# Two chained transformer blocks on one core: shift and scale slots by pairs, later first-stage products as rounded pairs

## Chip, core and metric

The kernel runs on one NeuronCore of a Trainium2 chip. The metric is the device time of one execution in microseconds (us). What the text calls engines: TensorE (PE; its weight loads are PEld), VectorE (DVE), ScalarE (ACT), GpSimd (POOL, nearly unused), and SyncE (SP), which here only issues DMA transfers of weights. The core has one PSUM, used as four units of two banks, and one SBUF.

## What is computed

Two blocks for 256 tokens of width 1024, in float32. The part that the change touches is the head of the first block: the modulation vectors, the first norm, and the product with `w_in`.

```python
cs = silu(c)
mod = cs @ mod_w + mod_b                       # six vectors of 1024
sh1, sc1, g1, sh2, sc2, g2 = split(mod, 6)
h = rms_norm(x, norm1_g) * (1 + sc1) + sh1
z = h @ w_in + b_in                            # queries, keys, values, gates, merge gates
...                                            # three attention branches from z
x = x + g1 * (merged @ w_out)
h = rms_norm(x, norm2_g) * (1 + sc2) + sh2
x = x + g2 * moe_ffn(h)                        # 32 experts, 4 per token
x = rms_norm(x, final_g)
...                                            # second block: adaln with 9 vectors for each of 2 layers,
                                               # ffn, neighbourhood attention, ffn, ffn, short convolution, ffn
```

## The kernel before

All activations of a stage lie transposed, 8 chunks of 128 features by 256 tokens (`xT`, `hT`). Weights stream through a ring of slots of 128 x 2048 float32 (1 MB each); `PLAN` writes down the order of the slots, which place of the ring each takes, and what releases that place. SP walks this list in order, and a slot whose place is not released holds up all behind it. In the first stage the ring has 9 places (`RING1`), then 7.

**Modulation slots.** 96 slots hold `mod_w`. Each carries two of the eight 128-row chunks of one vector. `mod_slot(i)` on VectorE multiplies the slot with the condition row (L1860, two instructions with an accumulated sum for one condition, four for two conditions), and after the fourth slot of a vector `modulation(n)` adds the bias, and for a scale the one and the norm's gain (L1879, L1881). The first eight slots are the shift and the scale of the first norm. The next twelve are put one behind each slot of the first stage, 8 in attention, 4 in the branch stage, the others in the feed-forwards of the second block.

**First stage.** `norm(0)`: ScalarE squares `xT` (L758), TensorE sums with a matrix of ones (L1306), ScalarE takes the root (L761). VectorE does eight modulation slots, the reciprocal (L1896), divides four chunks at once (L1936), and scales and shifts each (L1943). Then TensorE runs three passes z0, z1, z2 of 8, 8 and 5 output chunks (`Z_PASSES`) with plain float32 matmuls (`gemm`, L1180), each over 8 input chunks, 168 matmuls in all. VectorE brings each pass out of PSUM with the bias (L1966). Then come transposes of the value chunks ("vnat", L1334), four pieces of 2 output chunks each (`piece`, "zpiece0" to "zpiece3", L1345, 16 matmuls each), and between them the compression network (L1358 to L1407).

**Rounded products.** Later stages split a float32 operand into a rounded part (fp32r, "high", a ScalarE copy) and the rest ("low", a VectorE subtraction) and add three products: high x high, high x low, low x high. In attention the merge pieces do this (`split_piece`, L1468 to L1471; copies L850 and L2047), with `h1_high` (L798) and `h_low`, which lies on top of `hT` (L2052). The experts do it with L898 and L2276, and the second block with `split_gemm` (L1226, copies L1041 and L2412).

**After attention.** The branch stage multiplies each branch by `w_branch` (L1180), VectorE merges it (L2146 to L2151), then `w_out`, which VectorE adds to `xT` (L2167). After the experts, norm2 sums two products (L1306, L1308) with `gains2`, a 128 x 1024 table; VectorE needs its result at L2424.

Of the kernel before, what the change touches and what calls it, by code (L numbers as in the profile page):

```python
# [72 lines left out]
FIRST_VECS = VEC_AT["b_in"][0]  # L73
# [5 lines left out]
for _name, _width in CONSTS:  # L79
# [10 lines left out]
MODS = [(1, 0, g, 1) for g in range(6)] + \  # L90
       [(2, layer, g, 2 if (layer, g) < (0, 5) else 1)
        for layer in range(2) for g in ((0, 1, 2, 5, 6, 3, 7, 4, 8) if layer == 0 else range(N_MOD))]
# [34 lines left out]
class Plan:  # L127
# [3 lines left out]
    def __init__(self):  # L131
# [8 lines left out]
        self.split_at, self.split_no = [], {}  # L140

# [19 lines left out]

    def gemm(self, name, tensor, index, k_chunks, col0, cols, n_units, mods_every=0, mods_end=0, split=False,
             first=0):


# [3 lines left out]
        for k in range(0, k_chunks, 2):  # L169
            self.slots[name].append(len(self.stream))  # L170
# [5 lines left out]
            if split:  # L176
                self.split_no[len(self.stream)] = len(self.split_at)
                self.split_at.append(len(self.stream))
            self.stream.append((tensor, index, (k + first) % k_chunks, 2, col0, cols))
# [5 lines left out]
    def piece(self, name, z):  # L185

        self.unit(name)
        self.slots[name] = len(self.stream)
# [3 lines left out]
    def mod_slots(self, n):  # L192

        for _ in range(n):
            block_, layer, g, _ = MODS[self.n_mod_slots // 4]
            pair = self.n_mod_slots % 4
# [6 lines left out]
def make_plan():  # L203
    p = Plan()
    p.mod_slots(8)
    p.unit("norm0")
    for n, (c0, nc_) in enumerate(Z_PASSES):
        p.gemm(f"z{n}", "w_in", 0, DC, c0 * P, nc_ * P, 2, mods_every=1, mods_end=5)
    p.unit("vnat", 2)
    p.load("cmp_w1", [("cmp_w1", kv, 8 * half, 8, 0, 256) for kv in range(2) for half in range(2)])  # L210
    p.piece("zpiece0", 8)
# [3 lines left out]
    p.piece("zpiece1", 10)  # L215
    p.unit("cmp_hturn")
    p.piece("zpiece2", 12)
# [3 lines left out]
    p.piece("zpiece3", 14)  # L221
# [50 lines left out]
    p.unit("norm2")  # L272
    for e, (f, _) in enumerate(FFNS):
# [57 lines left out]
def square_parts(n):  # L331
# [3 lines left out]
    if n == 2:  # L335
        return PAIRS_OF
# [33 lines left out]
def build(nc, ins, out):  # L370
    with ExitStack() as ctx:
# [92 lines left out]
        gateT, b2_rows, gains2 = area(ARENA - T, T), cond_rows[:, 0, :], area(moe["h_nat_low"][0], D)  # L464
# [30 lines left out]
        w_low = sb_at("w_low", [P, RING2, SLOT], F32R, ring_at)  # L495
        w_high = sb_at("w_high", [P, HIGHS, SLOT], F32R, ring_at + 4 * RING2 * SLOT)
# [51 lines left out]
        def low_ap(s, cols):  # L548
            return w_low[:, PLAN.place[s], 0:2 * cols].rearrange("p (k n) -> p k n", k=2)

# [133 lines left out]
        def _(sp):  # L684
# [7 lines left out]
            stream(0, 3)  # L692
            sp.dma_start(xT[:, :, :], ins["xT"].rearrange("(k p) t -> p k t", p=P)).then_inc(sem("x_landed"), 16)
            stream(3, 10)
            sp.dma_start(vecs[:, FIRST_VECS:], ins["vecs"][:, FIRST_VECS:]).then_inc(sem("rest_landed"), 16)
            sp.dma_start(consts[:, P:], ins["consts"][:, P:]).then_inc(sem("rest_landed"), 16)
            stream(10, PLAN.moe_slot)
# [1980 lines left out]
```

## Time and profile before

| | us |
|---|---|
| median of 3 runs | 2763.68 (2761.77 to 2766.82) |
| the profiled execution, its own time | 2760.82 |
| span from first to last instruction | 2759.0 |
| PE busy | 2640.4 (96%) |
| DVE busy | 2096.0 (76%) |
| ACT busy | 1579.1 (57%) |
| mean granted TensorE clock | 0.98 |

The page cuts the span into 40 equal slices of 69 us. A digit is the busy share in tenths: PE shows 5 in the first slice and 9 in almost all that follow, with 8 in a few. A timeline row gives the start, the busy time of a run of instructions, engine, line and operation, and in square brackets how long the engine had been idle before it and what released it. A window row gives, for a stretch of time, the busy time of each engine, the granted clock (1.00 is 2.4 GHz, 0.50 is 1.2 GHz), the DMA share and GB/s. TensorE's float32 matmuls leave two records each.

### The profile page before, as it was taken

What the parts mean: (1) busy time and instruction counts of PE and PEld (TensorE: products, weight loads), DVE (VectorE), ACT (ScalarE), POOL (GpSimd) and SP (SyncE); (2) the same over time, 40 slices, a digit from 0 to 9 for tenths busy, and PEclk for the clock granted to TensorE, in tenths of its full rate; (3) what the DMA queues carried; (4) which work ended last, traced back from release to release, by engine and by line L of the source; (5) the groups of instructions that cost most, each with busy time, mean ns of one, the idle gap of its engine ahead of it and who ended that gap; (6) DMA issues with size and microseconds to landing.
All of it is one profiled execution on the core that took longest, in us unless ns stands there. A gap on an engine that the chain in (4) does not pass through costs nothing.

```text
span 2759.0 us, 43009 instructions
## 1 busy us (share of the span) xinstructions
PE 2640.4 (96%) x17218; PEld 2403.7 (87%) x17218; DVE 2096.0 (76%) x1998; ACT 1579.1 (57%) x1411; POOL 0.4 (0%) x6
## 2 busy tenths in 40 slices
PE   5999989999999999999998999999989999999998
PEld 4788878888888888888886999999879999999998
DVE  6357749999999999999997888785546866754553
ACT  1145328888888888888884443453434444442442
POOL 0000000000000000000000000000000000000000
PEclk9999999999999999999998999999999999999999
DMA  9844448999999999999995877777417867754551
GB/s 398 292 159 135 177 164 354 378 389 384 394 391 388 393 388 393 391 389 392 387 382 231 279 277 268 287 265 251 144 62 260 289 227 278 287 171 153 175 192 62
DMA packets 160816, 777.62 MB, mean 282 GB/s; under 512 B 12304, under 2 KB 38032, under 8 KB 97456
## 3 DMA queue, kind: packets, MB, share of 16 engines
q1 hardware_dynamic: 156352, 768.71, 73.0%
q10 hardware_dynamic: 4336, 7.05, 0.9%
q8 instruction: 99, 1.62, 0.2%
q14 instruction: 29, 0.24, 0.0%
HBM read 774.66 MB, written 1.05 MB: 281 GB/s over the span
## 4 chain that ended last, share of the span: by engine, by line
PE 79%; DVE 12%; issue 4%; ACT 3%; DMA 2%; SPq 0%; DVEq 0%; ACTq 0%
PE psum L1226 38%; PE psum L1578 18%; PE psum L1180 7%; DVE w_low L2276 6%; PE psum L1618 4%; PE psum L1555 2%; PE psum L1596 2%; ACT w_high L898 1%; PE psum L1306 1%; PE psum L1345 1%; DVE arena L2303 1%; PE psum L1393 1%; PE psum L1440 1%; DVE ring L1860 1%; PE psum L1468 1%
## 5 line engine op out<-in xcount | busy, mean ns | idle before, releaser
L2276 DVE TENSOR_TENSOR w_low<-ring,w_high 128x2048 fp32r<-128x2048 f32 x396 | 884.8, 2286 | 30.1 <-ACT w_high L898 17.7
L898 ACT ACTIVATE w_high<-ring 128x2048 fp32r<-128x2048 f32 x396 | 736.0, 1905 | 43.0 <-PE psum L1578 42.8
L1041 ACT ACTIVATE w_high<-ring 128x2048 fp32r<-128x2048 f32 (+1 forms) x199 | 362.4, 1829 | 527.8 <-PE psum L1226 409.6
L2412 DVE TENSOR_TENSOR w_low<-ring,w_high 128x2048 fp32r<-128x2048 f32 (+1 forms) x199 | 432.6, 2184 | 293.5 <-ACT w_high L1041 292.4
L1226 PE MATMUL psum<-h_high,w_high 128*128 128x256 f32 x2080 | 585.5, 282 | 20.9 <-ACT h_high L1054 20.8
L1226 PE MATMUL psum<-h_high,w_low 128*128 128x256 f32 x2080 | 592.4, 285 | 0.0
L1226 PE MATMUL psum<-h_low,w_high 128*128 128x256 f32 x2080 | 586.7, 284 | 0.0
L1226 PEld LDWEIGHTS psum<-h_high,w_high 128*128 128x128 f32 x2080 | 398.6, 192 | 23.2 <-issue 22.6
L1226 PEld LDWEIGHTS psum<-h_high,w_low 128*128 128x128 f32 x2080 | 394.8, 190 | 0.0
L1226 PEld LDWEIGHTS psum<-h_low,w_high 128*128 128x128 f32 x2080 | 394.1, 190 | 0.0
L1578 PE MATMUL psum<-w_high,xg 128*128 128x512 f32 x1056 | 295.8, 402 | 0.6 <-ACT xg L926 0.6
L1578 PE MATMUL psum<-w_low,xg 128*128 128x512 f32 x1056 | 291.4, 397 | 1.1
L1226 PE MATMUL psum<-m_high,w_high 128*128 128x256 f32 x880 | 245.9, 279 | 1.8 <-DVE arena L2447 1.8
L1860 DVE SCALAR_TENSOR_TENSOR ring<-ring,cond_rows 128x1024 f32<-128x1024 f32 x192 | 228.1, 1221 | 24.9 <-DMA ring<-in_mod_w 14.1
L1226 PE MATMUL psum<-m_high,w_low 128*128 128x256 f32 x880 | 246.2, 280 | 0.0
L1226 PE MATMUL psum<-m_low,w_high 128*128 128x256 f32 x880 | 246.1, 280 | 0.0
L1578 PEld LDWEIGHTS psum<-w_low,xg 128*128 128x128 f32 x1056 | 196.9, 188 | 55.5 <-DVE w_low L2276 8.2
L1578 PEld LDWEIGHTS psum<-w_high,xg 128*128 128x128 f32 x1056 | 196.5, 189 | 45.0 <-issue 0.8
L1578 PE MATMUL psum<-w_high,hid 128*128 128x512 f32 x528 | 152.2, 410 | 23.2 <-DVE hid L2319 23.2
L1226 PEld LDWEIGHTS psum<-m_high,w_high 128*128 128x128 f32 x880 | 165.4, 188 | 2.3 <-DVE arena L2447 2.3
L1226 PEld LDWEIGHTS psum<-m_high,w_low 128*128 128x128 f32 x880 | 165.4, 188 | 0.0
L1226 PEld LDWEIGHTS psum<-m_low,w_high 128*128 128x128 f32 x880 | 165.3, 188 | 0.1
(289 smaller groups left out, 3357.8 us busy)
## 6 DMA issues: line engine op xcount, KB each, us to landing
ring<-in_exp_w SPq DMA_DIRECT2D x396, 1024.0 KB, 8.6
ring<-in_ffn_w SPq DMA_DIRECT2D x135, 1024.0 KB, 5.6
ring<-in_mod_w SPq DMA_DIRECT2D x96, 1024.0 KB, 6.2
ring<-in_ffn_w SPq DMA_DIRECT2D x40, 768.0 KB, 4.9
ring<-in_w_in SPq DMA_DIRECT2D x24, 1024.0 KB, 9.6
ring<-in_even_w_in SPq DMA_DIRECT2D x12, 1024.0 KB, 7.3
ring<-in_conv_w_in SPq DMA_DIRECT2D x12, 1024.0 KB, 5.1
ring<-in_w_branch SPq DMA_DIRECT2D x6, 1024.0 KB, 5.0
```

The costliest lines, as they stand in the source:

```text
L898: act.activation(high_ap(j, D), slot_ap(PLAN.moe_slot + j), ACT.Copy).then_inc(sem("expert_high_ready" + c.x), 1)
L1041: act.activation(high_ap(m, cols), slot_ap(s, 2, cols), ACT.Copy).then_inc(sem("w_high_ready"), 1)
L1180: mm = pe.matmul(unit(u0 + j // 4)[:, (j % 4) * T:(j % 4 + 1) * T], w[:, k % 2, (c0 + j) * P:(c0 + j + 1) * P], rhs(k), start=(k == 0 and ...
L1226: return pe.matmul(unit(u0 + j // 4)[:, (j % 4) * T:(j % 4 + 1) * T], w[:, k % 2, j * P:(j + 1) * P], h[:, k, :], start=first, stop=stop, ...
L1306: mm = pe.matmul(unit(u)[:, 0:T], ones, squares[:, k, :], start=(k == 0), stop=(k == DC - 1))
L1555: mm = pe.matmul(cols[:, n, :, part * CAP:(part + 1) * CAP], h_nat[:, b, k * P:(k + 1) * P], sel[:, b, :, :], start=(b == 0), stop=(b == T ...
L1578: mm = pe.matmul(u[:, cols], x_parts(k), w[:, k % 2, cols], start=(k == 0 and w is wh), stop=(k == DC - 1 and w is wl), skip_group_check=True)
L1596: mm = pe.matmul(u[:, k * CAP:(k + 1) * CAP], moe_buf(rows)[:, k * P:(k + 1) * P], const("fold"), start=True, stop=True)
L1618: mm = pe.matmul(c.unit(name)[:, (k % 4) * T:(k % 4 + 1) * T], moe_buf(f"y_rows{e}")[:, k * P:(k + 1) * P], moe_buf(f"selT{e}"), start=(e ...
L1860: last = dve.scalar_tensor_tensor(to, w[:, j, :], 1.0, cond_rows[:, row, :], ALU.mult, ALU.mult, accum_out=sums)
L2276: dve.tensor_tensor(low_ap(PLAN.moe_slot + j, D), slot_ap(PLAN.moe_slot + j), high_ap(j, D).bitcast(F32), ALU.subtract).then_inc(sem("expe ...
L2412: dve.tensor_tensor(low_ap(s, cols), slot_ap(s, 2, cols), high_ap(m, cols).bitcast(F32), ALU.subtract).then_inc(sem("w_split"), 1)
```

## The change

Four edits, and their consequences for the ring and the order.

**Head.** The shift and scale slots are no longer vector by vector but pair by pair: slot 2p is the shift and slot 2p+1 the scale of input chunks 2p and 2p+1. Each slot is finished by its own small `modulation`, and chunk pair p of `hT` is divided, scaled and shifted right after it and signalled (`h0_parts`). A slot of z0 is streamed behind each two modulation slots. `xT` is now the first transfer on SP. On ScalarE the transfer of the condition comes third and not first; the squares come in four parts before the Silu, and a root of a constant is put ahead of the real one.

**z1, z2 and the four pieces** are three rounded products. Highs of weights are ScalarE copies into the places 9, 10 and 11 of the ring; lows are VectorE subtractions in the slot's own place (`early_lows`). `h1_high` is made in four parts behind `h0_parts`; `h_low` overwrites `hT`, so VectorE waits for the end of z0. Each low is written out at a fixed place of VectorE's order. zpiece0 moves ahead of the vnat transposes.

**Four modulation slots fewer** lie ahead of attention (16 and not 20). Attention keeps its 8, and the branch stage and `w_out` have 8 and not 4. The order of vectors is changed: the gate of the expert block now comes last of these and the second block's first two before it.

**gains2** moves to two other buffers in two halves; one of them is where slots with two conditions leave their products, and the first modulation slot of the second block comes three weight slots later (`since_mods = -2`).

```diff
-MODS = [(1, 0, g, 1) for g in range(6)] + \
+MODS = [(1, 0, g, 1) for g in range(5)] + [(2, 0, 0, 2), (2, 0, 1, 2), (1, 0, 5, 1)] + \
...
+MOD_SLOTS = [(i % 2, i // 2) if i < 8 else divmod(i, 4) for i in range(4 * len(MODS))]
...
 def make_plan():
     p = Plan()
-    p.mod_slots(8)
     p.unit("norm0")
     for n, (c0, nc_) in enumerate(Z_PASSES):
-        p.gemm(f"z{n}", "w_in", 0, DC, c0 * P, nc_ * P, 2, mods_every=1, mods_end=5)
+        p.gemm(f"z{n}", "w_in", 0, DC, c0 * P, nc_ * P, 2, mods_every=2, mods_end=4 if n else 0,
+               highs=((), (9, 10, 11, 9), (10, 11, 9, 10))[n], mods_before=0 if n else 2)
+    p.piece("zpiece0", 8, (9,))
...
+    p.since_mods = -2
...
-            act.dma_start(cond_rows[:, 0, :], ins["cond_rows"][0]).then_inc(sem("cond_landed"), 16)
             act.dma_start(vecs[:, 0:FIRST_VECS], ins["vecs"][:, 0:FIRST_VECS]).then_inc(sem("vecs_landed"), 16)
             act.dma_start(ones, ins["consts"][:, 0:P]).then_inc(sem("ones_landed"), 16)
...
+            act.dma_start(cond_rows[:, 0, :], ins["cond_rows"][0]).then_inc(sem("cond_landed"), 16)
...
+            act.wait_ge(sem("x_landed"), 16)
+            for some in PAIRS_OF:
+                some = slice(some[0], some[-1] + 1)
+                act.activation(hT[:, some, :], xT[:, some, :], ACT.Square).then_inc(sem("squares_ready"), 1)
+            act.wait_ge(sem("cond_landed"), 16)
+            act.activation(cond_rows[:, 0, :], cond_rows[:, 0, :], ACT.Silu).then_inc(sem("cond_ready"), 1)
+            act.wait_ge(sem("vecs_landed"), 16)
+            act.activation(small[:, 463:464], vec("eps")[:, 0:1], ACT.Sqrt)
+            sqrt_of_sums(0)
...
-            for n, (c0, nc_) in enumerate(Z_PASSES):
-                gemm(f"z{n}", DC, nc_, [(h_rhs, 0, nc_)], first_parts if n == 0 else None)
...
+            gemm("z0", DC, Z_PASSES[0][1], [(h_rhs, 0, Z_PASSES[0][1])], lambda k: pe.wait_ge(sem("h0_parts"), k // 2 + 1))
+            split_gemm("z1", DC, Z_PASSES[1][1], h1_high, h_low,
+                       lambda k: k % 2 or pe.wait_ge(sem("h1_low_ready"), k // 2 + 1),
+                       high_ready=lambda: pe.wait_ge(sem("h1_high_ready"), 1))
+            split_gemm("z2", DC, Z_PASSES[2][1], h1_high, h_low)
...
+            def early_lows(name, some=slice(0, None)):
...
+                    dve.wait_ge(sem("early_high_ready"), PLAN.early_no[s] + 1)
+                    high, low_ = early_parts(s, rows, cols)
+                    dve.tensor_tensor(low_, slot_ap(s, rows, cols), high.bitcast(F32), ALU.subtract).then_inc(
+                        sem("early_split"), 1)
```

VectorE at the head of the program, before: eight slots, then the root, then `hT` in two halves. `mod1` holds the modulation vectors of the first block, `cond_rows` the condition.

```order
L1860 SCALAR_TENSOR_TENSOR ring,mod1<-ring,cond_rows 128x1024 x8
L1879 TENSOR_TENSOR mod1<-mod1,vecs 128x8
L1860 SCALAR_TENSOR_TENSOR ring,mod1<-ring,cond_rows 128x1024 x8
L1879 TENSOR_TENSOR mod1<-mod1,vecs 128x8
L1881 SCALAR_TENSOR_TENSOR mod1<-mod1,vecs 128x8
L1896 RECIPROCAL rstd<-rstd 128x256
L1936 TENSOR_TENSOR hT<-xT,rstd 128x1024
L1943 TENSOR_SCALAR hT<-hT,mod1 128x256 x4
L1936 TENSOR_TENSOR hT<-xT,rstd 128x1024
```

The same place now:

```order
L1910 SCALAR_TENSOR_TENSOR ring,mod1<-ring,cond_rows 128x1024 x2
L1929 TENSOR_TENSOR mod1<-mod1,vecs 128x2
L1956 RECIPROCAL rstd<-rstd 128x256
L1910 SCALAR_TENSOR_TENSOR ring,mod1<-ring,cond_rows 128x1024 x2
L1929 TENSOR_TENSOR mod1<-mod1,vecs 128x2
L1931 SCALAR_TENSOR_TENSOR mod1<-mod1,vecs 128x2
L1999 TENSOR_TENSOR hT<-xT,rstd 128x512
L2001 TENSOR_SCALAR hT<-hT,mod1 128x256 x2
```

The first chunk pair stands behind two slots and not eight; the three other pairs follow it, each behind two slots of its own.

VectorE from the end of z0 on, before: nothing but modulation slots and the passes' way out of PSUM (`arena<-psum,vecs`).

```order
L1860 SCALAR_TENSOR_TENSOR ring,mod1<-ring,cond_rows 128x1024 x8
L1879 TENSOR_TENSOR mod1<-mod1,vecs 128x8
L1966 TENSOR_TENSOR arena<-psum,vecs 128x1024 x2
L1860 SCALAR_TENSOR_TENSOR ring,mod1<-ring,cond_rows 128x1024 x8
L1879 TENSOR_TENSOR mod1<-mod1,vecs 128x8
```

The same stretch now, from the first weight low of z1 (`ring_rounded`) to that of its last slot:

```order
L1950 TENSOR_TENSOR ring_rounded_56<-ring,ring_rounded_56 128x2048
L2009 TENSOR_TENSOR h_low_58<-hT,h1_high_62 128x512 x4
L1950 TENSOR_TENSOR ring_rounded_56<-ring,ring_rounded_56 128x2048
L2020 TENSOR_TENSOR arena<-psum,vecs 128x1024 x2
L1950 TENSOR_TENSOR ring_rounded_56<-ring,ring_rounded_56 128x2048
L2030 TENSOR_TENSOR vecs<-vecs 128x2x64
L2031 TENSOR_REDUCE small<-vecs 128x2
L2034 TENSOR_TENSOR small<-small 128x1
L2035 TENSOR_SCALAR small<-small 128x1
L2036 TENSOR_SCALAR vecs<-vecs 128x128
L1910 SCALAR_TENSOR_TENSOR ring,mod1<-ring,cond_rows 128x1024 x2
L1950 TENSOR_TENSOR ring_rounded_56<-ring,ring_rounded_56 128x2048
```

The lows, for which TensorE now waits, stand between the work that was there before.

VectorE at the last merge of the branches and at `w_out`, now (before, rows 1 and 5 of this piece were not there):

```order
L1910 SCALAR_TENSOR_TENSOR ring,mod1<-ring,cond_rows 128x1024 x4
L2230 TENSOR_TENSOR arena<-psum,ring 128x1024
L2232 TENSOR_TENSOR arena<-arena 128x1024
L2230 TENSOR_TENSOR arena<-psum,ring 128x1024
L2232 TENSOR_TENSOR arena<-arena 128x1024
L2256 MEMSET arena 128x2048
L2260 MEMSET small 128x1 x8
L1910 SCALAR_TENSOR_TENSOR ring,mod1<-ring,cond_rows 128x1024 x4
L1929 TENSOR_TENSOR mod1<-mod1,vecs 128x8
L2248 SCALAR_TENSOR_TENSOR xT<-psum,mod1,xT 128x256 x8
```

Two one-condition slots stand ahead of the last merge, and two more ahead of the addition of `w_out` (the last row).

## Rows read from the trace of the kernel before

**Rows 1.** The page's chain of work that ended last, shares by engine.

```profile
PE 79%; DVE 12%; issue 4%; ACT 3%; DMA 2%; SPq 0%; DVEq 0%; ACTq 0%
```

**Rows 2.** Windows of core 0: length, busy PE, PEld, DVE, ACT, POOL, clock, DMA, GB/s.

```profile
0.00:15.00 15.00, 0.00 (x0) 0.00 (x0) 4.93 (x9) 2.34 (x2) 0.20 (x4) 1.00 0.91 334
...
23.20:34.80 11.60, 0.00 (x0) 0.00 (x0) 11.05 (x19) 0.44 (x1) 0.00 (x0) 0.71 1.02 421
...
63.00:91.00 28.00, 28.00 (x131) 24.67 (x130) 12.42 (x20) 0.00 (x0) 0.00 (x0) 1.00 0.94 369
```

**Rows 3.** Timeline of the head: start, busy, engine, line, idle before.

```profile
7.42 1.06 ACT L741 ACTIVATE cond_rows<-cond_rows 128x1024 f32<-128x1024 f32 x1 [3.99 <-DMA cond_rows<-in_cond_rows]
10.07 1.23 DVE L1860 SCALAR_TENSOR_TENSOR ring<-ring,cond_rows 128x1024 f32<-128x1024 f32 x1 [10.07 <-DMA vecs<-in_vecs]
...
15.67 1.91 ACT L758 ACTIVATE hT<-xT 128x2048 f32<-128x2048 f32 x1 [7.19 <-DMA xT<-in_xT]
...
17.60 1.28 ACT L761 ACT_TABLE_LOAD   x1
...
17.73 5.40 PE L1306 MATMUL psum<-hT,consts 128*128 128x256 f32 x16 [17.73 <-ACT hT L758]
...
23.17 0.47 ACT L761 ACTIVATE rstd<-psum,vecs 128x256 f32<-128x256 f32 x1 [4.29 <-PE psum L1306]
...
28.04 1.23 DVE L1860 SCALAR_TENSOR_TENSOR ring<-ring,cond_rows 128x1024 f32<-128x1024 f32 x1
...
30.72 0.17 DVE L1881 SCALAR_TENSOR_TENSOR mod<-mod,vecs 128x8 f32<-128x8 f32 x1
30.92 1.75 DVE L1896 RECIPROCAL rstd<-rstd 128x256 f32<-128x256 f32 x1
...
32.82 1.23 DVE L1936 TENSOR_TENSOR hT<-xT,rstd 128x1024 f32<-128x1024 f32 x1
34.09 1.38 DVE L1943 TENSOR_SCALAR hT<-hT,mod 128x256 f32<-128x256 f32 x4
...
34.87 74.44 PE L1180 MATMUL psum<-hT,ring 128*128 128x256 f32 x336 [11.74 <-DVE hT L1943]
```

**Rows 4.** Chain of the first 110 us: start, length, what.

```profile
10.61 17.40 DMA ring<-in_mod_w
```

**Rows 5.** Windows of one microsecond in the head: the granted clock, ahead of DMA share.

```profile
28.00:29.00 1.00, 0.00 (x0) 0.00 (x0) 0.96 (x1) 0.00 (x0) 0.00 (x0) 0.51 1.07 426
...
38.00:39.00 1.00, 1.00 (x5) 0.88 (x4) 0.56 (x4) 0.90 (x2) 0.00 (x0) 0.87 1.08 434
```

**Rows 6.** Timeline at the end of z0 on DVE.

```profile
64.46 1.22 DVE L1966 TENSOR_TENSOR arena<-psum,vecs 128x1024 f32<-128x1024 f32 x1 [0.43 <-PE psum L1180]
```

**Rows 7.** Chain of the whole span: one feed-forward with rounded products.

```profile
2258.51 188.57 PE psum L1226 x1584
```

**Rows 8.** The page's groups: weight low and weight high of 128x2048.

```profile
L2276 DVE TENSOR_TENSOR w_low<-ring,w_high 128x2048 fp32r<-128x2048 f32 x396 | 884.8, 2286 | 30.1 <-ACT w_high L898 17.7
L898 ACT ACTIVATE w_high<-ring 128x2048 fp32r<-128x2048 f32 x396 | 736.0, 1905 | 43.0 <-PE psum L1578 42.8
```

**Rows 9.** Timeline of PE: zpiece0, compression network, zpiece3.

```profile
113.35 7.14 PE L1345 MATMUL psum<-hT,ring 128*128 128x256 f32 x32 [0.72 <-DMA ring<-in_w_in]
...
120.43 14.00 PE L1358 MATMUL psum<-ring,arena 128*31 128x256 f32 x64
...
153.14 8.86 PE L1345 MATMUL psum<-hT,ring 128*128 128x256 f32 x32
```

**Rows 10.** Timeline of DVE: last merge of the branches, first addition of `w_out`.

```profile
358.64 1.22 DVE L2149 TENSOR_TENSOR arena<-psum,ring 128x1024 f32<-128x1024 f32 x1 [8.81 <-PE psum L1180]
...
382.29 1.66 DVE L2167 SCALAR_TENSOR_TENSOR xT<-psum,mod,xT 128x256 f32<-128x256 f32 x4 [16.29 <-PE psum L1180]
```

**Rows 11.** Timeline at norm2: PE's last sums, then DVE's use of them.

```profile
1510.18 0.59 PE L1308 MATMUL psum<-hT,arena 128*128 128x256 f32 x2
...
1512.73 0.42 DVE L2424 TENSOR_SCALAR small<-psum 128x256 f32<-128x256 f32 x1
```

More of the change, by code:

```diff
@@ L214, in make_plan @@
         p.released[p.slots["cmp_w1"] + s] = ("units", p.n_units)
-    p.piece("zpiece1", 10)
+    p.piece("zpiece1", 10, (10,))
+    p.mod_slots(1)
     p.unit("cmp_hturn")
-    p.piece("zpiece2", 12)
+    p.piece("zpiece2", 12, (9,))
+    p.mod_slots(2)
     p.unit("cmp_kv")
@@ L220, in make_plan @@
     p.unit("cmp_scores")
-    p.piece("zpiece3", 14)
+    p.piece("zpiece3", 14, (10,))
+    p.mod_slots(1)
+    assert p.n_mod_slots == 16
     p.placed()
@@ L1335, in _ @@
                 mm.then_inc(psum_full, 1)
-            def piece(name):
-                u, s = U[name], PLAN.slots[name]
-                open_unit(pe, u)
-                await_slot(pe, s)
-                w = slot_ap(s, DC, 2 * P)
-                for k in range(DC):
-                    for j in range(2):
-                        mm = pe.matmul(unit(u)[:, j * T:(j + 1) * T], w[:, k, j * P:(j + 1) * P], hT[:, k, :],
-                                       start=(k == 0 and j == 0), stop=(k == DC - 1), skip_group_check=True)
-                mm.then_inc(psum_full, 1)
-            piece("zpiece0")
             pe.wait_ge(sem("blocks_ready"), 1)
@@ new lines, in _ @@
+            for part, some in enumerate(PAIRS_OF):
+                if part:
+                    mod_slot(2 * part)
+                    mod_slot(2 * part + 1)
+                two = slice(some[0], some[-1] + 1)
+                link(dve.tensor_tensor(hT[:, two, :], xT[:, two, :], rstd[:, 0:1, :].broadcast_to([P, 2, T]), ALU.mult))
+                for k in some:
+                    last = dve.tensor_scalar(hT[:, k, :], hT[:, k, :], mod1[:, 1, k:k + 1], mod1[:, 0, k:k + 1],
+                                             ALU.mult, ALU.add)
+                last.then_inc(sem("h0_parts"), 1)
@@ new lines, in _, with z_pass @@
+            early_lows("z1", slice(0, 1))
+            await_unit(dve, U["z0"] + 1)
+            for part, some in enumerate(PAIRS_OF):
+                two = slice(some[0], some[-1] + 1)
+                dve.wait_ge(sem("h1_high_ready"), part + 1)
+                dve.tensor_tensor(h_low[:, two, :], hT[:, two, :], h1_high[:, two, :].bitcast(F32),
+                                  ALU.subtract).then_inc(sem("h1_low_ready"), 1)
+            early_lows("z1", slice(1, 2))
+            def z_pass(n):
+                c0, nc_ = Z_PASSES[n]
+                for half in range(-(-nc_ // 4)):
+                    u, k = U[f"z{n}"] + half, min(4, nc_ - 4 * half)
+                    z = c0 + 4 * half
+                    await_unit(dve, u)
+                    last = dve.tensor_tensor(zT[:, z:z + k, :], chunks(u, k), wide(vec("b_in")[:, z:z + k], T), ALU.add)
+                    if half == 0:
+                        free(last, u)
+                finish(last, u, "z_ready")
@@ L1981, in _ @@
             last.then_inc(sem("blocks_ready"), 1)
+            early_lows("zpiece1")
+            mod_slot(12)
+            early_lows("zpiece2")
+            mod_slot(13)
+            mod_slot(14)
             u = U["cmp_hidden"]
@@ L1989, in _ @@
                 sem("cmp_bias_ready"), 1)
+            early_lows("zpiece3")
+            mod_slot(15)
             u = U["cmp_kv"]
```

235 lines of the change are left out of this document (134 added, 101 removed).

## The prediction

> **What bounds the kernel now.** I read the page's chain first: 79% of what ended last is TensorE's, 12% VectorE's [rows 1]. A gain has to take time from TensorE, or start it earlier. The windows say where that is possible. Up to 34.8 us TensorE does only the sums of the first norm (5.40 us from 17.73); VectorE is busy 11.05 of 11.60 us in 23.2:34.8 while DMA runs full at 421 GB/s [rows 2, 3]. From 63 to 91 us TensorE is busy 28.00 of 28.00 [rows 2]. So the head is bound by modulation slots, and the passes by TensorE itself.
>
> What comes after the first stage is the same work in the same order, but for two places named below. So whatever the first stage gains should arrive at the end unchanged, if nothing later waits for DMA; TensorE's chain carries that part.
>
> **Head of the kernel: when z0 can start.** Before, the eighth slot's data land at 10.61 + 17.40 = 28.01 us [rows 4], the ninth MB on SP's queue (eight slots and xT, which is fourth). xT landed at 15.67 [rows 3], so five further MB took 12.34 us, 2.47 us each. In the new order xT is MB 1, slots 0 and 1 are MB 2 and 3, and slots 6 and 7 are MB 10 and 11, z0's last weights MB 12. Counted back from 28.01, they land near 8.3, 10.7, 13.2 and 30.5, 33.0, 35.4 us. For xT, 334 GB/s over the first 15 us [rows 2], with its own 1.05 MB and the 0.6 MB of ScalarE's transfers, gives 4.9 us plus the start of some 2; I take 7.5, with bounds of 6.5 and 8.3.
>
> Then ScalarE: four squares, together a little above the 1.91 us of the one before, say 2.4, to 10.0; a table load of 1.28 and the Silu of 1.06 [rows 3], to 12.4. Before, the Silu began at 7.42 and VectorE's first slot at 10.07 [rows 3], so this edit moves VectorE's start 2.3 us later. The condition is now the third small transfer; it landed at 7.42 as the first, and would cost nothing up to 10.0. TensorE's sums run 5.40 us beside this, from 8.2 to 13.6, and the root is out at 14.3.
>
> VectorE: a slot with both operations took 30.92 - 28.04 = 2.88 us, one without the second 0.20 less (30.92 - 30.72), 2.68 [rows 3]. Slot 0: 12.4 to 15.1. Reciprocal, 32.82 - 30.92 = 1.90: to 17.0. Slot 1: to 19.85. Division of two chunks and two chunks scaled: half of 1.23 + 1.38 [rows 3] and 0.1 for the waits, 1.4: to **21.3 us**, where z0 starts. Before it was 34.87 [rows 3]: **13.6 us earlier**.
>
> Does z0 then run through? Each further pair costs VectorE 2.68 + 2.88 + 1.4 = 7.0 us, so pairs are ready at 28.3, 35.3 and 42.3 us; their slots have landed by then (33.0 and 35.4 for the last two). z0's 64 matmuls took 64.4 - 34.87 = 29.5 us (the end from [rows 6], 0.06 before that row), 7.4 us a pair. TensorE is hardly ahead of VectorE, and the waits are below 1 us. The 29.5 us hold a slow start already: the granted clock had fallen to 0.51 at 28 us, five microseconds after the sums, and was back at 38 to 39 us (0.87) [rows 5]; the idle time here is of the same kind, 13.6 to 21.3. So z0 ends at 50.8.
>
> **z1 and z2 as three rounded products.** Before: 34.87 + 74.44 = 109.3 [rows 3], less 64.4, is 44.9 us for 104 matmuls, 0.432 us each. In a feed-forward 1584 rounded matmuls take 188.57 us, 0.119 each [rows 7]. Three times 104 of these is 37.1 us: **7.8 us less**. This holds only if the parts are ready. A high is 1.91 us and a low 2.29 us per slot [rows 8], against 48 x 0.119 = 5.7 us of matmuls per slot of z1 and 3.6 of z2. VectorE's work from the end of z0 to the low of zpiece0: h_low 2.4, three lows of z1 6.9, two exits 5.2, the lambda step 1.7, four slots 9.9, four lows of z2 (five eighths wide) 5.7, one low 2.3, in all 34 us in 37. Followed in the written order, with times from z0's end: low of z1 slot 1 is ready at 4.8 and needed at 5.7; slot 2 at 9.7 and 11.4; slot 3 at 16.2 and 17.0; z2's first at 20.0 and 22.8, its third at 27.5 and 29.9. All in time, but three times with less than 1 us to spare. zpiece0 isn't: its high must wait for place 9, held by z2's third slot until 33.5, then 1.9 and 2.3, so ready at 37.9 against 37.1. **Cost 0.8 us.** Lower bound 0; upper bound 5 us, if each VectorE step takes a tenth more than its row and one wait turns up.
>
> SP's queue: each slot's place is released at least one slot's transfer ahead of its use; the second-last slot of z2 is behind modulation slot 11, which waits for slot 8 to be used (some 14 us after z0's end), and lands near 20, needed at 33. No DMA wait.
>
> **The pieces.** zpiece0 took 7.1 us, now 48 x 0.119 = 5.7. Before, 120.43 - 109.3 = 11.1 us lie between z2's end and the compression network [rows 3, 9]; of these 7.1 are the piece, 2.0 the vnat transposes, 2.0 waits for z2's exit and for a slot. With the piece ahead of the transposes these waits are covered: 0.8 + 5.7 + 2.0 = 8.5 instead of 11.1, which holds the 0.8 already, **2.6 us less**. The network itself stays at 14.0 [rows 9] and hides two lows and three slots of VectorE. zpiece1 and zpiece2: 1.4 less each, **2.8 us**. Before the compressed keys VectorE now has a low and a slot more; it comes there some 0.3 to 1 us late, **cost 0.3**. zpiece3 took 8.86 [rows 9], 1.7 more than zpiece0 for the same matmuls; I keep the 1.7 and take 5.7 + 1.7, **1.4 less** (1.4 to 3.1).
>
> h_low's 2.3 us on VectorE ahead of the first merge piece disappear, but the low of that piece waited for ScalarE's copy, not for it: nothing.
>
> **Branch stage.** Four slots with one condition, 4 x 2.4 = 9.6 us of VectorE, and 4 MB. Two go ahead of the last merge, where VectorE waited 8.81 us, two ahead of the addition, where it waited 16.29 us [rows 10]. 4.8 us fit into each: nothing, and 4.8 if the first cover were gone. The slots that SP loads behind them have their places 1 to 9 us before TensorE asks.
>
> **norm2.** TensorE's sums end at 1510.18 + 0.59 = 1510.8; VectorE takes them at 1512.73 [rows 11], because a two-condition slot (four instructions of 1.2 us) lies between its lows. That slot comes later now: **1.9 us less**, 0 at worst. Moving gains2 adds one short instruction, which hides in the wait for the last expert's rows.
>
> **The sum.** 13.6 + 7.8 + 2.6 + 2.8 - 0.3 + 1.4 + 1.9 = 29.8 us. The profiled execution took 2760.82 us (span 2759.0), so it would be 2731.0. The median of the runs is 2763.68, 2.9 above; there the same gain gives **2734 us**.
>
> **A rule of the skill against the row.** The square ends at 15.67 + 1.91 = 17.58 us and the table load behind it runs from 17.60 for 1.28 us [rows 3]; the switch shows no more than that, and the sum uses it. The Trainium skill, "ScalarE Activation LUTs", section "What ACT_TABLE_LOAD costs", states about 2.66 us for every switch to another set, a drain included. One such load now stands ahead of the Silu, hence ahead of all of VectorE: by the page the sum would be 28.4 and the time 2735.3. An estimate from the page; it changes no chance.
>
> **Rivals.**
> *The parts come late (chance 0.15).* VectorE is filled 34 of 37 us in z1 and z2, and every low is behind something. For it: the three margins below 1 us, and that a wait for ScalarE's exponential sits in the middle. Against it: each duration is one that repeats within 1% on the page. If each of some ten steps loses 0.5 us and the head starts 1.5 us later, 6.5 us go: 2740.
> *More than forecast (0.08).* xT and the condition land by 6.5 us (1.0), zpiece3 keeps the full clock (1.7) and the slow start of z0 is shorter (1.0): 2730.
> *The clock stays at half (0.03), the one that ends slower.* In z0 TensorE waits for VectorE pair by pair. If these waits kept the granted clock at 0.5 as at 28 us [rows 5], z0 would take 27.6 us more (64 x 0.432), and if it went on, z1 and z2 37.1 more: 2734 + 64.7 = 2799. It decides against the change from 60 us of such work on (30 us lost). Against it: a pair's 7.0 us of VectorE is below TensorE's 7.4, so that the gaps nearly vanish. The Trainium skill, "TensorE: Matmul & The Clock Gate", section "HAM oscillation — how this bites in real kernels", describes a kernel that falls back at each wait for a tile; here that would be this rival.
> *It doesn't do what it says (0.04).* The head's start is set by something in the first 20 us that I don't see (the condition landing last, at 15 us or later, or the eight slots still arriving first), and only the matmul part is left: 29.8 - 13.6 = 16.2, so 2747.5.
>
> **How the numbers follow.** Forecast 0.70. Its own range is 2730 to 2738: -1.7 for zpiece3, -1 for xT and -1.5 for the scatter of a median (runs lie within 3.1 of it) in part together; +1.5 for xT and +2 for late parts. 8 times in 10 needs half of the first rival as well: 2729 to 2741. Faster by over 0.2% (5.5 us, about what a measurement of this kernel can tell): all but the clock rival and a rest for a hazard of the branch stage, 0.95; within 0.2% 0.02; slower 0.03.
>
> **What would show it.** z0's first matmul near 21.3 us and its exit on VectorE at 50.8; squares from 7.5; the pass matmuls 0.119 us apart; z2's end near 88, the compression network from 96.6, zpiece3's end near 134 where it was 162.0; the merge and addition rows still with idle time before them; L2424's successor straight behind TensorE's sums. Wrong would be: TensorE waiting over 2 us in z1 or z2 for a low (first rival), a granted clock of 0.5 in z0 after its fourth microsecond (clock rival), z0 starting after 25 us (last rival), or idle time gone before the last merge.

## The result, and the profile after

The changed kernel takes 2734.86 us (median of 4 runs, 2730.78 to 2737.13); beside it the kernel before takes 2764.16 us. The ratio is 0.9892, 95% interval 0.9880 to 0.9904: 29.3 us or 1.1% faster, forecast 29.8. The profiled execution took 2736.34 us with a span of 2734.5, so 24.5 us less span than before; why this pair of profiles shows less than the medians is answered below.

The timeline of the head after the change (start, busy, engine, line, idle before and what ended it), which answers to [rows 3]:

```profile
6.67 2.19 ACT L794 ACTIVATE hT<-xT 128x512 f32<-128x512 f32 x4 [3.04 <-DMA xT<-in_xT]
8.87 1.28 ACT L796 ACT_TABLE_LOAD   x1
9.57 5.90 PE L1366 MATMUL psum<-hT,consts 128*128 128x256 f32 x16 [9.57 <-DMA consts<-in_consts]
13.32 1.06 ACT L796 ACTIVATE cond_rows<-cond_rows 128x1024 f32<-128x1024 f32 x1 [3.17 <-DMA cond_rows<-in_cond_rows]
14.41 1.23 DVE L1910 SCALAR_TENSOR_TENSOR ring<-ring,cond_rows 128x1024 f32<-128x1024 f32 x1 [14.41 <-ACT cond_rows L796]
...
17.09 1.75 DVE L1956 RECIPROCAL rstd<-rstd 128x256 f32<-128x256 f32 x1
18.99 1.23 DVE L1910 SCALAR_TENSOR_TENSOR ring<-ring,cond_rows 128x1024 f32<-128x1024 f32 x1
...
23.39 2.93 PE L1230 MATMUL psum<-hT,ring 128*128 128x256 f32 x6 [7.91 <-DVE hT L2001]
```

xT lands at 6.67 as hoped, but the ones land at 9.57 and the condition at 13.3, with the table long there: ScalarE waits 3.17 us for it. VectorE starts at 14.41 and works through to z0, which starts at 23.39: 11.5 us earlier than 34.87.

The windows of the changed kernel (length, busy PE, PEld, DVE, ACT, POOL, granted clock, DMA share, GB/s) cover z0's first 4.6 us, the rest of z0, and z1 with z2; they answer to [rows 2, 5]:

```profile
23.40:28.00 4.60, 4.60 (x12) 3.74 (x13) 4.46 (x8) 0.59 (x1) 0.00 (x0) 0.54 0.99 409
28.00:53.40 25.40, 25.40 (x120) 22.38 (x119) 17.49 (x36) 7.51 (x6) 0.00 (x0) 1.00 1.02 415
53.40:90.60 37.20, 37.16 (x312) 36.90 (x311) 31.61 (x38) 10.44 (x8) 0.00 (x0) 1.00 0.99 355
```

TensorE is busy all through z0, although it gets its chunks pair by pair. The granted clock is 0.54 for 4.6 us, near the lower of the two levels (1.2 and 2.4 GHz), then full to the end. z1 and z2 are 312 matmuls in 37.2 us, full and without a gap.

The chain of waits of the changed kernel from there on (start, length, what):

```profile
23.39 29.99 PE psum L1230 x128
53.38 33.63 PE psum L1286 x282
87.03 1.93 ACT ring_rounded L812
89.05 2.30 DVE ring_rounded L1950
...
99.12 13.93 PE psum L1422 x64
...
136.92 1.75 PE psum L1480 x16
```

The one wait of the passes is zpiece0's, through the high that needs place 9 and the low behind it, and TensorE's own waits put it at 0.8 us:

```profile
PE psum L1392 <- DVE ring_rounded L1950: 0.8, 1, 0.8
```

Zpiece3 ends at 136.9, where it was 162.0 [rows 9]: 25.1 us earlier. Later marks on TensorE's chain, before and after: first branch matmul 317.65 and 295.48, sums of norm1 389.07 and 366.88, first matmul of the first feed-forward 1517.10 and 1494.53, next norm 1653.19 and 1628.06, the norm after that 1845.49 and 1818.86.

VectorE at the last merge and at the addition of `w_out`, and at norm2 (timeline; answers to [rows 10, 11]):

```profile
336.44 1.23 DVE L2230 TENSOR_TENSOR arena<-psum,ring 128x1024 f32<-128x1024 f32 x1 [4.07 <-PE psum L1230]
...
360.09 1.66 DVE L2248 SCALAR_TENSOR_TENSOR xT<-psum,mod,xT 128x256 f32<-128x256 f32 x4 [11.30 <-PE psum L1230]
...
1490.14 0.42 DVE L2508 TENSOR_SCALAR small<-psum 128x256 f32<-128x256 f32 x1 [3.21 <-PE psum L1368]
```

Idle time is left before merge and addition, and from the first branch matmul to norm1 it is 71.4 us before and after. At norm2 VectorE now waits for TensorE instead of the reverse.

### The profile page after: what moved, and what is told of

It is laid out like the page before. It is cut to its first block, busy times and chain, and to the rows that moved or that the text cites. A ratio compares the mean times of both kernels' runs of the same rounds, so it can differ in the third digit from the quotient of the medians.

```text
span 2734.5 us, 43413 instructions
## 1 busy us (share of the span) xinstructions
PE 2633.9 (96%) x17386; PEld 2406.5 (88%) x17386; DVE 2121.5 (78%) x2025; ACT 1603.1 (59%) x1431; POOL 0.4 (0%) x6
## 4 chain that ended last, share of the span: by engine, by line
PE 82%; DVE 10%; issue 3%; ACT 3%; DMA 1%; DVEq 0%; PEld 0%; ACTq 0%; PEldq 0%
PE psum L1286 41%; PE psum L1629 19%; DVE w_low L2357 6%; PE psum L1230 6%; PE psum L1669 4%; PE psum L1606 2%; PE psum L1647 2%; PE psum L1366 1%; ACT w_high L948 1%; PE psum L1392 1%; PE psum L1395 1%; PE psum L1394 1%; PE psum L1457 1%; PE psum L1504 1%; DVE arena L2387 1%
```

## The experiments

Eleven further runs were made: nine altered kernels, and the two kernels of the comparison once more. Times are medians; beside each other they carry an uncertainty of several us (the 95% interval of a ratio is some 0.002 to each side, 5 us), so differences below that are read from the traces.

**1. Twice the same: what differs between two profiles?** `again` is the changed kernel, `before_again` the one before, both unaltered.

> The changed kernel, unaltered, once more. In its first profile the stretch from the end of zpiece3 to the first branch matmul took 158.7 us where the kernel before took 155.8, with a granted clock of 0.74 in two windows of 20 us where before had 0.83. Theory A (the dips of the clock in this stretch differ from execution to execution): the stretch is between 155 and 160 us and differs from 158.7 by more than 1 us. Theory B (the stage now begins at another moment, and this costs 2.9 us every time): 158.7 within 0.5. Median 2735 by both; z0 starts at 23.4 and the condition lands at 13.3.

> The kernel before, unaltered, for a second profile. The stretch from the end of zpiece3 to the first branch matmul took 155.8 us in its first profile; in eight profiles of kernels that have this stretch unchanged but begin it at other moments it took 156.5 to 160.2. Theory A (scatter between executions, by where the clock dips): now between 156 and 160, more than 0.5 from 155.8. Theory B (the change costs some 2 us here): 155.8 within 0.4. From the last sum of norm2 to the feed-forward's first matmul 6.9 us, and from there to the next norm 135.8 to 136.1, by both.

`again`: 2735.51 us (5 runs), z0 at 23.62, the condition at 13.5. The stretch from the end of zpiece3 to the branches took 293.88 - 136.47 = 157.4 us against 158.6 in the first profile. In `before_again` it took 323.60 - 163.30 = 160.3, against 155.7 in the first profile of that kernel. Its chain, the two marks:

```profile
163.30 1.75 PE psum L1416 x16
...
323.60 14.08 PE psum L1180 x64
```

So theory A, with a value just above its range in `before_again`: the kernel before itself ranges over 4.7 us there, and the change costs nothing that these profiles can show. In all thirteen profiles the stretch follows the mean granted clock in it: 155.8 us at 0.92, 155.8 to 156.5 at 0.91, 157.6 at 0.90, 158.7 at 0.89, 160.3 and 160.5 at 0.88 (counted from TensorE's first matmul behind zpiece3). What shifts the dips of the clock from one execution to the next stays open. In all, the profile used for the forecast was a quick one (span 2759.0; `before_again` 2766.7). One more expectation failed: norm2 took 5.0 us in `before_again`, not 6.9 (experiment 6).

**2. Head undone alone.**

```
+    p.mod_slots(8)
     p.unit("norm0")
...
-            mod_slot(0)
+            for i in range(8):
+                mod_slot(i)
             root(0)
-            mod_slot(1)
```

> Undoes the head alone: all eight slots are streamed and reduced before the root and the first chunk pair, as before; xT stays first, the passes and pieces stay in rounded products. Theory (head and passes add up, and the head is worth what z0's start shows): the eighth slot lands at 6.7 + 8 x 2.47 = 26.4 us, z0 starts at 26.4 + 2.9 + 1.9 + 1.4 = 32.6 to 33, 9.4 us later than 23.4, and the time is 9.4 above the changed kernel: 2744. Rival (VectorE, filled in z1 and z2, gives part of it back, since z0 no longer ends on its heels): 6 to 7 us above, 2741 to 2742.

Measured 2750.51 us (4 runs, 2744.28 to 2752.05), 15.0 above `again`. z0 starts at 40.48, not 33. The timeline of this kernel:

```profile
14.54 1.22 DVE L1911 SCALAR_TENSOR_TENSOR ring<-ring,cond_rows 128x1024 f32<-128x1024 f32 x1 [14.54 <-ACT cond_rows L797]
...
37.06 1.75 DVE L1957 RECIPROCAL rstd<-rstd 128x256 f32<-128x256 f32 x1 [0.33 <-DVE mod L1932]
...
40.48 29.59 PE L1231 MATMUL psum<-hT,ring 128*128 128x256 f32 x128 [25.34 <-DVE hT L1999]
```

VectorE starts at 14.54 and is filled to 36.7: 22.2 us for eight slots, 2.8 each, never waiting for a slot. I had taken the landings as the limit; with the condition this late it is VectorE. And from z0's first matmul to z1's first it takes 29.2 us with everything ready, against 29.3 to 30.6 in the ten profiles that feed it pair by pair: the pairs cost at most 1.3 us. Neither theory had the size. That the gain arrives at the end is in keeping with the times (z0's end 16.7 later than in the first profile, 15.6 later than in `again`, the median 15.0), though four runs that spread over 7.8 us could hide a loss of a few us.

**3. Rounded products undone alone.** z1, z2 and the pieces as in the kernel before, the rest as changed.

```
-            split_gemm("z1", DC, Z_PASSES[1][1], h1_high, h_low,
...
-            split_gemm("z2", DC, Z_PASSES[2][1], h1_high, h_low)
+            gemm("z1", DC, Z_PASSES[1][1], [(h_rhs, 0, Z_PASSES[1][1])])
+            gemm("z2", DC, Z_PASSES[2][1], [(h_rhs, 0, Z_PASSES[2][1])])
```

> Undoes the rounded products alone: z1, z2 and the four pieces multiply whole numbers in one product each, with the head, the order of the pieces and the mod slots of the changed kernel. Theory (the prediction's terms): z1 and z2 take 44.9 us instead of 37.1, each piece 1.4 us more (the last up to 3.1), the 0.8 us wait of zpiece0 goes: 12.6 to 14.3 us above the changed kernel, 2747.5 to 2749. Rival (the compression part is bound by VectorE, so that faster pieces give nothing): 7 to 8 us above, 2742.5.

Measured 2747.38 us (4 runs), 11.9 above `again`. zpiece0 runs from 97.60 in its chain:

```profile
97.60 6.91 PE psum L1399 x32
104.51 1.75 PE psum L1409 x16
106.25 13.93 PE psum L1420 x64
```

From the start of the compression network to the end of zpiece3 it takes 41.5 us, where the rounded pieces take 37.8 and 36.3. From z1's first matmul to that network it takes 53.6 us, with rounded products 46.0. That is 7.6 us from the passes and 3.7 to 5.2 from the pieces; the median came out just under the theory's 12.6 to 14.3, and far above the rival's 7 to 8: pieces give their time too.

**4. What limits the head.** Three kernels change nothing but the transfers of the ones and the condition. `cond_first` has the condition first on ScalarE's queue; `ones_on_chip` writes the matrix of ones with one instruction of 0.2 us; `cond_behind_x` puts the condition behind xT on SP's queue.

```
-            act.dma_start(ones, ins["consts"][:, 0:P]).then_inc(sem("ones_landed"), 16)
+            pool.memset(ones, 1.0).then_inc(sem("ones_landed"), 16)
```

> The condition's transfer goes first on ScalarE's queue, as in the kernel before, and not third. Theory (its late landing, 13.3 us, is what the prediction missed in the head): it lands by 8 us, the Silu follows the table load at 10.2, slot 0 runs from 11.3 to 14.0, then the root, for which TensorE's sums set the time (out at 15.7 to 16.3), is the last to arrive: reciprocal to 18.1, slot 1 to 21.0, z0 starts at 22.4, one microsecond earlier than 23.4; the time 2734. Rival (slot 0 or the vectors or ones land later than the condition, so it doesn't matter): z0 starts at 23.4 or later, the time 2735 or more. If the prediction's 14.3 us for the root were right, z0 would start at 21.

> One part of the earlier head alone: the matrix of ones is written on chip at 0.7 us instead of loaded; the condition stays the last transfer on ScalarE's queue, behind the vectors. Theory (two things end together in the head, VectorE's chain behind the condition and TensorE's sums behind the ones; taking one away gives little): the sums start at 7.4 and the root is out before 14.5, but slot 0 still starts only when the condition is there, at 13.3 + 1.1 or a few tenths earlier; z0 starts at 23.0 to 23.4. Rival (the sums are the limit): z0 starts at 20.5 to 21.5, 2 to 3 us below the changed kernel.

> The other part alone: the condition goes right behind xT on SP's queue; the ones are still loaded on ScalarE's. Theory: it lands near 8, the table load still ends at 10.2, slot 0 runs from 11.2 to 13.9; the ones land at 9.6 or a little earlier, the sums end at 15.3 and the root is out at 15.8 to 16.3: reciprocal to 18.0, slot 1 to 20.9, z0 starts at 22.3, 1.1 us earlier than the changed kernel, 2734. Rival (the condition alone is the limit): z0 starts at 20.3, 3 us earlier, 2732.

`cond_first`: 2733.17 us (5 runs), z0 at 23.90, half a microsecond later, not one earlier. xT landed at 8.4 and the ones at 10.6, in its timeline:

```profile
10.59 6.00 PEld L1366 LDWEIGHTS psum<-hT,consts 128*128 128x128 f32 x16 [10.59 <-DMA consts<-in_consts]
...
17.60 1.75 DVE L1956 RECIPROCAL rstd<-rstd 128x256 f32<-128x256 f32 x1 [1.97 <-ACT rstd L771]
```

With 0.5 MB moved ahead, what TensorE's sums need came later, and the root became the limit: VectorE waits 1.97 us for it. `ones_on_chip`: 2731.17 us (4 runs), z0 at 20.97. My expectation was wrong and the rival's number right, though not for its reason: without the 64 KB ahead of it the condition landed at 10.9 instead of 13.3, so that this edit shortened both waits. `cond_behind_x`: 2730.18 us (4 runs), z0 at 22.16, as worked out (22.3). Here the condition waits for nothing, but the sums run from 8.52 for 6.74 us, and VectorE stands 1.95 us for the root. The three medians cannot be told apart, nor surely from the changed kernel's. The starts of z0 can: each wait hides behind the other, and in both kernels that start z0 at 21 us or earlier both had shrunk (`ones_on_chip` and the one of experiment 5).

**5. An earlier head in full, and other places for the highs of the pieces.** The ones as in `ones_on_chip`, the condition as in `cond_behind_x`, and:

```
-    p.piece("zpiece0", 8, (9,))
+    p.piece("zpiece0", 8, (11,))
...
+            act.activation(small[:, 463:464], vec("eps")[:, 0:1], ACT.Silu)
             act.wait_ge(sem("x_landed"), 16)
...
             mod_slot(0)
+            mod_slot(1)
             root(0)
-            mod_slot(1)
```

> The changed kernel with an earlier head, and another place for one weight high. The matrix of ones is written on chip instead of loaded; the condition goes on SP's queue right behind xT; a Silu on one column stands ahead of the squares, so that the table is there; slot 1 goes ahead of the reciprocal; the highs of zpiece0 to zpiece3 lie in places 11, 9, 10, 9. Theory (the head waits for small transfers, and the shift arrives at the end): squares 6.7 to 8.9, Silu to 10, slot 0 from 10.4, slot 1 to 16.0, sums from 7.3 to 13, reciprocal to 17.9, z0 starts at 19.3, 4.1 us earlier than 23.4; zpiece0 no longer waits 0.8 us; the time is 4.9 us below the changed kernel, 2730.5. Rival (the small transfers were not the limit, the slots are): slot 0 lands after 12, z0 starts at 21 or later, the time is 2733 or more.

Measured 2727.72 us (5 runs, 2726.32 to 2730.12), ratio to the kernel before 0.9877 (0.9858 to 0.9896), 7 us below the changed kernel's medians; the nine runs of the changed kernel lie from 2729.63 to 2737.13, so that the two sets touch only at their ends. Its timeline and chain:

```profile
8.81 1.04 ACT L798 ACTIVATE cond_rows<-cond_rows 128x1024 f32<-128x1024 f32 x1
9.87 1.28 ACT L799 ACT_TABLE_LOAD   x1
10.61 1.23 DVE L1911 SCALAR_TENSOR_TENSOR ring<-ring,cond_rows 128x1024 f32<-128x1024 f32 x1 [10.61 <-DMA ring<-in_mod_w]
...
19.59 6.62 PE L1231 MATMUL psum<-hT,ring 128*128 128x256 f32 x17 [6.47 <-DVE hT L2002]
...
50.16 37.42 PE psum L1287 x312
```

z0 starts at 19.59 (expected 19.3), now behind slot 0's landing; zpiece0 waits no more, and zpiece3 ends at 131.3, 5.1 to 5.6 earlier. That was worked out; the 2 us by which the median fell further are not accounted for. This is the best kernel of the study.

**6. The slot behind norm2 put back.**

```
     p.unit("norm2")
-    p.since_mods = -2
...
-            return rstd[:, :, :].rearrange("p a t -> p (a t)") if half == 0 else mod_junk[:, :].bitcast(F32)
+            return area(moe["h_nat_low"][0] + half * D // 2, D // 2)
```

> Undoes the move of the modulation slot behind norm2: the slot stands between the first weight lows again, as before, and so do the slots of the first feed-forwards behind it; the row vector of the gains goes back to its old place. Theory (the prediction's term): from TensorE's last sum of norm2 to the first matmul of the feed-forward 1.9 us more. In the traces the old rhythm also had 2.6 us more up to the next norm and 1.5 up to the one after, with two waits of 6 and 7 us that the chain puts down to weight transfers; if these belong to the slots' rhythm, they come back: 1.9 + 2.6 + 1.5 = 6 us above the changed kernel, 2741. Rival (they are scatter between executions): 1.9 above, 2737.

Measured 2738.06 us (6 runs), 2.6 to 3.2 above the changed kernel: between the two, and within what the runs scatter. The traces say more. From the start of norm2's last sum to the first matmul of the feed-forward it took 7.43 us; in the changed kernel and all its variants with the new rhythm 5.02. TensorE's timeline here:

```profile
1488.67 0.59 PE L1367 MATMUL psum<-hT,arena 128*128 128x256 f32 x2
1496.10 0.55 PE L1285 MATMUL psum<-h_high,w_high 128*128 128x256 f32 x1 [6.84 <-ACT h_high L1103]
```

From that matmul to the next norm: 136.09, 135.82 and 135.81 us in the three profiles with the old rhythm, 132.3 to 134.3 in the ten with the new one. From there to the norm after it took 190.8 to 191.9 us in either rhythm (192.3 and 192.2 in the kernel before): so the 1.5 us by which it differs between the first two profiles are not the rhythm's; where they come from stays open. The windows from first feed-forward to next norm, of the kernel before, the changed one and this one:

```profile
1517.10:1653.19 136.09, 134.61 (x1104) 134.02 (x1105) 114.92 (x131) 63.00 (x48) 0.00 (x0) 0.98 0.80 279
```

```profile
1494.53:1628.06 133.53, 133.18 (x1104) 132.81 (x1105) 114.86 (x128) 63.07 (x48) 0.00 (x0) 0.99 0.80 274
```

```profile
1496.10:1631.91 135.81, 133.44 (x1104) 132.66 (x1105) 114.61 (x131) 63.10 (x48) 0.00 (x0) 0.99 0.81 279
```

TensorE is idle 1.48 us of this in the kernel before, 1.66 in `before_again` and 2.37 here; with the new rhythm it is 0.35 in the changed kernel and at most 0.64 in any profile. What it waits for stands among its waits in this kernel; the changed kernel has no wait of either kind there:

```profile
PE psum L1285 <- DVE w_low L2495: 1.3, 2, 1.1
PE psum L1285 <- DVE arena L2530: 0.6, 1, 0.6
```

Waits of these two kinds come to 0.8 us in the first profile of before, 1.2 in the second and 1.9 here: with the modulation slots between them, VectorE's lows and its way out of PSUM are late for TensorE. The clock at the start of the feed-forward does not explain the difference, though it suggests itself from the first two profiles (granted 0.77 in the first 12.9 us before, 0.87 after). Here are these first 12.9 us in this kernel, which took 135.8 us all the same, and in `again`, which took 133.9:

```profile
1496.10:1509.00 12.90, 12.90 (x96) 12.69 (x96) 12.64 (x24) 8.52 (x10) 0.00 (x0) 0.89 0.63 119
```

```profile
1492.16:1505.06 12.90, 12.90 (x89) 12.90 (x90) 12.65 (x24) 8.51 (x10) 0.00 (x0) 0.80 0.63 118
```

The rest of the difference is TensorE's busy time, which by itself goes from 132.0 to 133.7 us among the kernels with the new rhythm.

In `before_again` norm2 took only 5.0 us: its sums had started later beside VectorE's lows, and more of them at the lower clock, so that VectorE was there first. The 1.9 us are paid only when the sums are early and quick.

**7. More VectorE work in z1.**

> Two more reductions of 1.23 us in modulation slot 8, 2.5 us of VectorE ahead of the low of z1's last slot. In the changed kernel's trace this low is ready at 68.85 us and TensorE, at 5.7 us a slot from 53.4, needs it at 70.5: a margin of 1.6. Theory (the margins are real and small): TensorE waits once, 0.9 us, in z1, nothing more comes up in z2 and zpiece0's wait of 0.8 stays; about 0.9 us later at zpiece3's end. Rival 1 (the chain of lows carries every delay on): 2.5 us and several waits. Rival 2 (there is more room than I think): no wait, 0.

```
+                if i == 8:
+                    for j in range(2):
+                        for c, row in enumerate(rows):
+                            link(dve.scalar_tensor_tensor(mod_junk[:, :], w[:, j, :], 1.0, cond_rows[:, row, :], ALU.mult,
+                                                          ALU.mult, accum_out=small[:, 461:462]))
```

Measured 2733.49 us (4 runs), no difference that a median can show. TensorE's waits can, and they are the theory's:

```profile
PE psum L1392 <- DVE ring_rounded L1955: 0.9, 1, 0.9
PE psum L1286 <- DVE ring_rounded L1955: 0.8, 1, 0.8
```

One new wait of 0.8 us (forecast 0.9), and the end of zpiece3 1.0 later than in the first profile. The margin of 1.6 took up 1.7 of the 2.5 us; the later lows passed on no more than the 0.1 us by which zpiece0's wait grew.

**8. More VectorE work in the branch stage.** The same edit with `28 <= i < 32`.

> Every reduction of the last four modulation slots ahead of norm1 (two ahead of the last merge of the branches, two ahead of the addition of w_out) is done twice: 5.0 us of VectorE more at each place. Idle in the changed kernel ahead of these: 4.07 and 11.30 us. Theory (this work hides until the idle time is used up): the merge comes 0.9 us late, and w_out with it; the addition is not late: 0.9 us from the first branch matmul to norm1. Rival (the slots' ring places come free later, so weights land late and TensorE waits for DMA): 3 us or more. If moving these slots had cost anything at once, merge and addition would both be late by 5.

Measured 2734.52 us (4 runs). The stretch from the first branch matmul to norm1 took 367.79 - 295.49 = 72.3 us against 71.4: 0.9, as expected. The last merge follows its slots without idle time, and the addition still waits (timeline):

```profile
361.00 1.66 DVE L2253 SCALAR_TENSOR_TENSOR xT<-psum,mod,xT 128x256 f32<-128x256 f32 x4 [6.24 <-PE psum L1230]
```

## Why the prediction was right, and where it was not

**The total** was 29.8 us, measured 29.3 between medians. It was so close partly by luck: a miss in the head (2.1 us too much) and a gain that was not foreseen (2.6 us) nearly cancel.

- **Head: right in kind, the term mis-sized.** 11.5 us, not 13.6. xT's landing (7.5, measured 6.7), the squares and table load, the 2.7 to 2.9 us of a slot and the 1.4 us of a pair held. The step that failed is "it landed at 7.42 as the first, and would cost nothing up to 10.0": as third, behind the ones, it landed at 13.3. The root, put at 14.3, was a second miss that the first one hid: the sums began at 9.6 and not 8.2, because of the ones, and took 5.9 us (6.7 in `again`) and not 5.4. With the condition out of the way and the sums at 8.5 the root is out at 15.8 and z0 starts at 22.2, still not at 21.3 (`cond_behind_x`).
- **z0 30.0 us instead of 29.5**: the slow start was there, as in [rows 5]. In `again` it was 30.8.
- **Slips in the working that changed nothing.** The order of the slots makes slots 6 and 7 the 11th and 12th MB of SP's queue, not the 10th and 11th; the landings used for them, 33.0 and 35.4, are those of the right count. And of the five margins that the prediction lists for the lows two are below 1 us (0.9 and 0.8), not three.
- **z1 and z2: 37.2 us, forecast 37.1.** No wait in them. The margin of z1's last low was 1.6 us, not 0.8: it was ready 15.5 us after z0's end, where my order of events had 16.2, and needed at 17.1. zpiece0's wait was 0.8 us, as forecast, by the cause forecast.
- **Pieces.** From z2's end to the compression network 8.5 us, forecast 8.5. From there to the end of zpiece3 37.8 us against 41.6 before, 3.8 less, forecast 2.8 - 0.3 + 1.4 = 3.9. In `again` it took only 36.3, see below the list.
- **Branch stage: nothing, as forecast**, and experiment 8 shows where the cover ends: 4.07 us of it are left at the merge.
- **norm2: 1.9 us**, the difference of the two profiles (6.92 and 5.02), but not in every execution: the second profile of before lacks it.
- **Missed: 2.6 us in the first feed-forward** (136.1 and 133.5), at least in part from the same shift of the slots (experiment 6). The prediction said that what comes after was the same work in the same order but for two places; the slots' places in this feed-forward had moved too.

The 1.5 us by which the pieces differ between the first profile and `again` lie in zpiece3. A window of two microseconds inside it, in the one and in the other, shows the lower clock and the full one:

```profile
131.00:133.00 2.00, 2.00 (x12) 2.00 (x11) 1.42 (x6) 0.41 (x1) 0.00 (x0) 0.50 0.96 368
```

```profile
131.00:133.00 2.00, 2.00 (x20) 2.00 (x19) 1.43 (x5) 1.31 (x8) 0.00 (x0) 1.00 1.00 408
```

So the 1.7 us that the prediction kept for this piece are a stretch at half clock that comes in some executions and not in others: of the ten profiles with rounded pieces, six have a mean clock of 0.75 to 0.88 in the last 5.6 us of zpiece3, and four have 1.00; without it the piece gains 2.9 us, near the prediction's other bound of 3.1.

With these terms: 11.5 - 0.5 + 7.7 + 2.6 + 3.8 + 1.9 + 2.6 = 29.6 us, beside 29.3. That the two agree so well proves less than it seems, for the seven terms come from one pair of profiles, and that pair differs by 24.5 us. Its other stretches make up the 5.1 us: attention 2.9 longer, norm1 to norm2 (the experts) 1.5 longer, all that lies behind the second norm of the second block 2.1 longer, and 1.4 shorter between the first and the second of these norms. The first three lie within the scatter of the thirteen profiles (experts 1120.3 to 1125.4 us, and 1121.3 and 1125.4 in the two executions of the kernel before; the last stretch 912.3 to 917.4) and are left out of the sum for that; no run shows that the change has no share in them.

Undone singly, head, rounded products and slot gave 15.0, 11.9 and about 2.9. That sums to 29.8, but by chance: with the head undone z0 starts 17.1 us later than in the changed kernel, 5.6 us more than the change had gained there, because the late condition stays in it.

**The rivals.** Parts that come late: one wait of 0.8 us, already in the sum. The clock at half: in z0 for 4.6 us only, never in z1 or z2 of the changed kernel. The falling back at each wait for a tile, which the Trainium skill, "TensorE: Matmul & The Clock Gate", section "HAM oscillation — how this bites in real kernels", describes, did not come: VectorE's 6.93 us a pair kept TensorE without a gap, so that no run here shows what such waits would have done. "It doesn't do what it says" named the right event, a condition that lands last, with 13.3 us where it wanted 15: 2.1 us came of it, not 13.6.

**The table load.** In `cond_behind_x` the load starts at 8.89 and takes 1.28 us, and the Silu starts at 10.19: the switch costs 1.30 us, where the row had promised 1.28. The 2.66 us of the Trainium skill, "ScalarE: Activation LUTs", section "What ACT_TABLE_LOAD costs", do not appear; the measurement decides. In the changed kernel itself the load hid behind the condition.

**Profile against medians.** 24.5 us of span against 29.3: the profiled execution of before was 2.9 us below its median and that of the changed kernel 1.5 above its own, and attention alone, 2.9 us longer in the profile after, varies by 4.7 us between two executions of the kernel before.

## What to carry to other kernels

When an engine's first work is moved ahead, list everything that it needs, small constants too, and ask of each what shares the DMA queues with it; a transfer's landing time read in one order need not hold in another (the condition landed at 7.4, 10.9 and 13.3 us). Where two waits run side by side, removing one gives less than its length, and only a trace of that kernel says how much. And read a term from two profiles of the same kernel before resting 2 us on it: here attention and norm2 differed by 4.7 and 1.9 us between two executions. A cause that fits two profiles should be held against all the others on hand: the clock at the start of the feed-forward fitted the first two, and `norm2_slot` and `again` speak against it.

## What was not expected of the hardware

- A 64 KB transfer ahead of the condition on the same queue went with a landing at 13.3 instead of 10.9 us while SP's queue moved 1 MB pieces (0.6 us of it is the later issue); the 64 KB themselves, issued at 1.2 us, landed at 9.6.
- With 0.5 MB moved to the front of the second queue, the 1 MB at the front of the first landed at 8.4 us (one profile), and at 6.5 to 7.0 in the other ten profiles with xT first.
- Unchanged code, executed again, differed by 4.7 us in a stretch of 160 us, and the time went with the mean granted clock of the stretch (0.92 and 0.88 in the two profiles of before; 0.74 in 235:275 of one profile of the changed kernel). zpiece3 alone, 48 matmuls, differed by 1.5 us in the same way between two executions of the changed kernel.
